# Hyena filters made in the modulation's stage and kept in DRAM until the convolutions

## The reference

```python
def hyena_kernel_fft(L, fw1, fb1, freq, fw2, fb2, fw3):
    hdn = jnp.sin(freq * (feats @ fw1 + fb1))
    hdn = jnp.sin(freq * (hdn @ fw2 + fb2))
    h = (hdn @ fw3).reshape(L, HY_ORDER, 2, HY_W)
    h = h * jnp.exp(-t[:, :, None, None] * jnp.abs(deltas))
    k = jnp.concatenate([h[:, :, 0], zeros, h[:0:-1, :, 1]], axis=0)
    k = k / (jnp.sum(jnp.abs(k), axis=0, keepdims=True) + EPS)
    return jnp.fft.rfft(k, axis=0)

def token_mixer(h, ...):
    u = centred_dwconv(h @ w_in[:, :HY_PROJ], ...); v, *gates = jnp.split(u, 3, axis=-1)
    kf = hyena_kernel_fft(L, ...)
    z = v
    for o, gate in enumerate(gates):
        z = gate * (fft_conv(z, kf[:, o]) + z * hy_bias[o])
    ...

mod = jax.nn.silu(c) @ w_ada + b_ada        # six parts of 2048; also for c_ctx
hc = rmsnorm(h_ctx, norm1_w) * (1.0 + csc1) + csh1
hl = rmsnorm(x, norm1_w) * (1.0 + sc1) + sh1
```

## Time and profile before

| | us |
|---|---|
| median of 3 runs | 4280.64 |
| lowest, highest | 4276.46, 4289.01 |
| the profiled execution | 4285.37 |
| its span, first to last instruction | 4283.6 |
| PE busy | 3877.2 (91%) |
| VectorE busy | 2815.2 (66%) |
| ScalarE busy | 2064.3 (48%) |
| GpSimd busy | 203.6 (5%) |

### The profile page before, as it was taken

The page is one execution under the profiler, slowest core; times in us unless marked ns, Lnnn a source line. Parts: engine busy times, 40 slices in busy tenths (PEclk is TensorE's granted clock), DMA queues, the critical chain, the costliest instruction groups (busy, mean ns, idle before and its releaser), DMA issues. The chain is left out here.

```text
span 4283.6 us, 66352 instructions
## 1 busy us (share of the span) xinstructions
PE 3877.2 (91%) x22156; PEld 3171.7 (74%) x22156; DVE 2815.2 (66%) x5280; ACT 2064.3 (48%) x3828; POOL 203.6 (5%) x242
## 2 busy tenths in 40 slices
PE   6699968778999999887699998998799999999998
PEld 0467744567888888774588877877688888888887
DVE  0553435777888667679686557687966666666667
ACT  0442330235666555455455434444955555555554
POOL 3011100000000000103100000000000000000000
PEclk9899979988999999998899999999999999999999
DMA  9686720034766666441255535555066665666665
GB/s 340 230 302 248 264 92 0 1 106 152 214 214 211 190 188 189 153 150 60 99 177 185 180 110 167 168 184 184 5 200 205 203 203 186 188 189 187 190 189 159
DMA packets 199380, 735.10 MB, mean 172 GB/s; under 512 B 22903, under 2 KB 22936, under 8 KB 197400
## 3 DMA queue, kind: packets, MB, share of 16 engines
q1 hardware_dynamic: 173992, 639.97, 47.6%
q0 software_dynamic: 25200, 92.64, 5.9%
HBM read 715.74 MB, written 16.78 MB: 171 GB/s over the span
## 5 line engine op out<-in xcount | busy, mean ns | idle before, releaser
L207 DVE TENSOR_TENSOR weights_lo<-ring,weights_hi 128x512 fp32r<-128x512 f32 x2240 | 1528.0, 695 | 978.1 <-ACT weights_hi L200 962.5
L200 ACT ACTIVATE weights_hi<-ring 128x512 fp32r<-128x512 f32 x2240 | 1396.4, 630 | 1373.9 <-PE ps L846 1308.4
L846 PE MATMUL ps<-expert_parts,weights_hi 128*128 128x512 f32 x4224 | 1466.9, 395 | 34.3 <-DVE weights_lo L207 26.8
L846 PE MATMUL ps<-expert_parts,weights_lo 128*128 128x256 f32 x4224 | 1142.6, 281 | 0.0
L846 PEld LDWEIGHTS ps<-expert_parts,weights_hi 128*128 128x128 f32 x4224 | 780.7, 189 | 205.2 <-issue 36.4
L846 PEld LDWEIGHTS ps<-expert_parts,weights_lo 128*128 128x128 f32 x4224 | 797.7, 189 | 20.4
L846 PE MATMUL ps<-mlp_parts,weights_hi 128*128 128x512 f32 x1024 | 354.0, 394 | 16.7 <-PEq L604 15.8
L846 PE MATMUL ps<-hidden,weights_hi 128*128 128x512 f32 x1024 | 351.5, 392 | 0.6 <-DVE weights_lo L207 0.6
L846 PE MATMUL ps<-mlp_parts,weights_lo 128*128 128x256 f32 x1024 | 277.4, 281 | 0.0
L846 PE MATMUL ps<-h_parts,weights_hi 128*128 128x512 f32 x704 | 266.1, 406 | 11.8 <-DVE weights_lo L207 11.8
L846 PE MATMUL ps<-hidden,weights_lo 128*128 128x256 f32 x1024 | 276.3, 280 | 0.0
(11 more groups left out here) (460 smaller groups left out, 4972.7 us busy)
## 6 DMA issues: line engine op xcount, KB each, us to landing
ring<-in_w_mlp SPq DMA_DIRECT2D x256, 512.0 KB, 3.7
ring<-in_w_u SPq DMA_DIRECT2D x256, 512.0 KB, 4.1
ring<-in_w_v_tab SPq DMA_DIRECT2D x256, 512.0 KB, 3.7
ada_ring<-in_w_ada POOLq DMA_DIRECT2D x124, 512.0 KB, 6.5
ring<-in_w_mix SPq DMA_DIRECT2D x88, 512.0 KB, 5.6
ada_ring<-in_w_ada SPq DMA_DIRECT2D x68, 512.0 KB, 5.2
ring<-in_w_out SPq DMA_DIRECT2D x64, 512.0 KB, 3.7
ring<-in_w_in SPq DMA_DIRECT2D x48, 512.0 KB, 4.0
```

What stands on the lines that cost most here:

```text
L200: act.activation(core.hi[:, g % SLOTS], core.ring[:, slot, at:at + QUARTER], ACT.Copy).then_inc(core.rounded, 1)
L207: dve.tensor_tensor(core.lo[:, g % SLOTS], core.ring[:, slot, at:at + QUARTER], core.hi[:, g % SLOTS].bitcast(F32), ALU.subtract).then_inc ...
L846: mm = pe.matmul(out, part[:, g % SLOTS, k, :], moving, start=at == 0 and part is core.hi, stop=last and part is core.hi)
```

## The change

The filters move from their own stage, between `dt_stage` and the convolutions, into `start_stage`, and are kept in a DRAM tensor until the convolutions.

- `FilterWork` holds the filter's work. Its loads (feats, w1, w2, w3 of both orders, window, dft) are issued on GpSimd's queue ahead of the other five. PE's part is a generator of 30 pieces: two for the network, then per order two of taps (four matmuls each, into PSUM banks 0 to 3, the second waiting until VectorE has windowed the first), two sums of magnitudes (banks 7 and 0) and ten spectra (banks 1 to 3 in turn). `first_steps` says after which of the 32 steps of the modulation each piece runs. VectorE's part is as before. ScalarE does sines, magnitudes and the copies of the modulation, and issues five stores of 512 KB per order (`spill`) to `filters_saved`, those of order 0 behind the copy of part 0, those of order 1 behind the copy of part 1.
- The buffers lie in space that later stages use: two tiles of 8192 columns, and parts of `u`, `xbc`, `xbc_ctx` and `zg`. ctx now lies in `u`, and the squares' scratch has a tile of its own. ScalarE waits at the stage's end for the stores of order 0 and, before its first work of the projections (`first_scalar`), for those of order 1.
- The block that loaded dft and inverse and `filter_stage` are gone; so is ScalarE's copy of one plane (L1097). In `dt_stage` SyncE issues two transfers of 1 MB from `filters_saved` into the modulation's ring (`early`). In the first `hyena_stage` it issues dft, two planes of 512 KB, inverse, and six planes of order 1 (`rest`). PE waits for dft ahead of its spectra and for inverse ahead of its way back, VectorE for the order's filters ahead of its products.

```diff
 class ModulationBeside(Beside):
+    def first_scalar(self, act):
+        self.filt.wait_spilled(act, 1)
...
-def start_stage(core, mod, ctx_tile, const_loads, scratch, squares):
+def start_stage(core, mod, ctx_tile, const_loads, scratch, squares, filt):
+    first_steps = (2, 5, 8, 9, 11, 12, 13, 13, 14, 15, 15, 16, 17, 17, 18, 19, 20, 21, 23, 24, 25, 25, 26, 27, 27, 28, 29, 29, 30, 31)
+    due = lambda n: sum(at <= n for at in first_steps)
...
-            for part in range(2):
-                mod.copy(act, part)
+            filt.sines(act)
+            filt.sizes(act, 0)
+            mod.copy(act, 0)
+            filt.spill(act, 0)
+            filt.sizes(act, 1)
+            mod.copy(act, 1)
+            filt.spill(act, 1)
+            filt.wait_spilled(act, 0)
         def _(pool):
+            filt.load(pool)
...
+            dve.wait_ge(loaded, 16)
+            filt.vector(dve)
             for part in range(2):
                 mod.finish(dve, part, 1)
...
         def _(pe):
+            pieces = filt.tensor(pe)
+            def after_step(n):
+                for _ in range(due(n) - due(n - 1)):
+                    next(pieces)
             for k in range(KD):
                 mod.multiply(pe, 0, k)
+                after_step(k)
             pe.wait_ge(tables, 16 * (3 + len(const_loads)))
             for k in range(4):
                 mod.multiply(pe, 1, k)
+                after_step(KD + k)
             mod.turn(pe, 0)
             for k in range(4, KD):
                 mod.multiply(pe, 1, k)
+                after_step(KD + k)
+            for _ in pieces:
+                pass
             mod.turn(pe, 1)
...
+class FiltersBack:
+    def early(self, sp):
+        back = self.filters_back[0]
+        sp.dma_start(self.ring[:, 0:2], self.saved[0, :, 0:2]).then_inc(back, 16)
+        sp.dma_start(self.ring[:, 2:4], self.saved[0, :, 3:5]).then_inc(back, 16)
+    def rest(self, sp):
+        dram = self.core.dram
+        sp.dma_start(self.dft[:], dram["dft"]).then_inc(self.dft_back, 16)
+        for n, plane in ((0, 2), (1, 1)):
+            sp.dma_start(self.pairs[0][KN0][:, n], self.saved[0, :, plane]).then_inc(self.filters_back[0], 16)
+        sp.dma_start(self.inverse[:], dram["inverse"]).then_inc(self.inverse_back, 16)
+        for first, n, plane in ((KA0, 0, 0), (KA0, 1, 1), (KN0, 0, 2), (KN0, 1, 1), (KB0, 0, 3), (KB0, 1, 4)):
+            sp.dma_start(self.pairs[1][first][:, n], self.saved[1, :, plane]).then_inc(self.filters_back[1], 16)
...
+    def tensor(self, pe):
...
+        for o in range(2):
+            if o:
+                pe.wait_ge(s["stored"], 2 * self.KINDS)
+            for t in range(TT):
+                if t:
+                    pe.wait_ge(s["windowed"], TT * o + t)
+                for a in range(2):
+                    for c in range(2):
+                        mm = pe.matmul(ps[:, 2 * a + c, :], space.hdn[:, t * P:(t + 1) * P],
+                                       space.w3[o][:, a, c * BANK:(c + 1) * BANK], start=True, stop=True)
+                mm.then_inc(s["taps"], 1)
+                yield
+            pe.wait_ge(s["tapped"], o + 1)
+            for c, bank in enumerate((7, 0)):
+                pe.wait_ge(s["abs"], 2 * o + c + 1)
+                for j in range(4):
+                    mm = pe.matmul(ps[:, bank, :], core.ones[:], space.tmp[:, j, :], start=j == 0, stop=j == 3)
+                mm.then_inc(s["abs_sum"], 1)
+                yield
...
+                for c in range(2):
+                    m = 2 * n + c
+                    if m >= 3:
+                        pe.wait_ge(s["stored"], 2 * self.KINDS * o + m - 2)
...
+                    mm.then_inc(s["spectrum"], 1)
+                    yield
+    def spill(self, act, o):
+        for n, plane in enumerate(self.space.planes[o]):
+            act.wait_ge(self.done["stored"], 2 * self.KINDS * o + 2 * n + 2)
+            act.dma_start(self.saved[o, :, n], plane).then_inc(self.spilled[o], 16)
...
 def hyena_stage
...
                 pe.wait_ge(s["token"], after["token"] + 4)
+                pe.wait_ge(back.dft_back, 16)
...
+                pe.wait_ge(back.inverse_back, 16)
...
+            @block.sync
+            def _(sp):
+                if o == 0:
+                    back.rest(sp)
...
+                dve.wait_ge(back.filters_back[o], back.landings[o])
```

More of the change, by code:

```diff
@@ L920, in dt_stage @@
         with nc.Block() as block:
+            @block.sync
+            def _(sp):
+                back.early(sp)
             @block.tensor
@@ new lines, with __init__ @@
+class FilterSpace:
+    def __init__(self, first, second, u, xbc, zg, xbc_ctx):
+        planes = lambda t: t.rearrange("p n t -> p (n t)")
+        self.taps = first[:, 0:4 * HY].rearrange("p (t a c) -> p t a c", t=TT, a=2)
+        self.tmp = first[:, 4 * HY:6 * HY].rearrange("p (j c) -> p j c", j=4)
+        self.norm = first[:, 6 * HY:7 * HY]
+        self.w1, self.w2 = first[0:33, 7 * HY:7 * HY + 64], first[0:64, 7 * HY + 64:7 * HY + 128]
+        self.hdn = first[0:64, 7 * HY + 128:7 * HY + 128 + T]
+        self.window = second[:, 0:TT * HY].rearrange("p (t c) -> p t c", t=TT)
+        self.dft = second[:, 2 * HY:2 * HY + TT * 6 * P].rearrange("p (t n m) -> p t n m", t=TT, n=6)
+        split = lambda t: t[0:64].rearrange("p (a c) -> p a c", a=2)
+        ctx_planes = planes(xbc_ctx)
+        self.w3 = split(second[:, 4 * HY:6 * HY]), split(ctx_planes[:, 0:2 * HY])
+        pair = lambda t: planes(t).rearrange("p (t c) -> p t c", t=TT)
+        self.even = pair(u[:, 16:24, :]), pair(zg)
+        self.planes = ([second[:, 6 * HY:7 * HY], second[:, 7 * HY:8 * HY], planes(xbc[:, 2:6, :]),
+                        self.even[0][:, 0], self.even[0][:, 1]],
+                       [ctx_planes[:, n * HY:(n + 1) * HY] for n in range(3)] + [self.even[1][:, 0], self.even[1][:, 1]])
@@ new lines, with __init__, make_room @@
+class FiltersBack:
+    def __init__(self, core, saved, ring):
+        self.core, self.saved, self.ring = core, saved, ring
+        self.dft_back, self.inverse_back = core.sem("dft_loaded"), core.sem("inverse_loaded")
+        self.filters_back = [core.sem(f"filters_back{o}") for o in range(2)]
+    def make_room(self, sb):
+        self.dft, self.inverse = sb("dft", [P, TT, 6, P]), sb("inverse", [P, 4, T])
+        last, later = sb("filters_last", [P, 2, HY]), sb("filters_later", [P, 6, HY])
+        self.pairs = ({KA0: self.ring[:, 0:2], KB0: self.ring[:, 2:4], KN0: last[:]},
+                      {n: later[:, n:n + 2] for n in (KA0, KN0, KB0)})
+        self.landings = 64, 96
+    def early(self, sp):
[10 more added lines that the diff above has]
+            sp.dma_start(self.pairs[1][first][:, n], self.saved[1, :, plane]).then_inc(self.filters_back[1], 16)
@@ L1139, in hyena_stage @@
-def hyena_stage(core, o, u, dft, inverse, filters):
+                        ins = dve.tensor_tensor(h[:, t, a, at], ps[:, 2 * a + c, :], space.window[:, t, at], ALU.mult)
+                ins.then_inc(s["windowed"], 1)
+            dve.wait_ge(s["windowed"], TT * (o + 1))
+            dve.memset(h[0:1, 0, 1, :], 0.0).then_inc(s["tapped"], 1)
+            dve.wait_ge(s["tapped"], o + 1)
+            dve.tensor_tensor(even, h[:, :, 0, :], h[:, :, 1, :], ALU.add).then_inc(s["even_odd"], 1)
+            dve.wait_ge(s["abs"], 2 * o + 2)
@@ new lines, in vector @@
+            dve.tensor_tensor(h[:, :, 1, :], h[:, :, 0, :], h[:, :, 1, :], ALU.subtract).then_inc(s["even_odd"], 1)
+            for c, bank in enumerate((7, 0)):
+                at = slice(c * BANK, (c + 1) * BANK)
+                dve.wait_ge(s["abs_sum"], 2 * o + c + 1)
+                step(dve.tensor_scalar(norm[:, at], ps[:, bank, :], EPS, None, ALU.add))
+                step(dve.reciprocal(norm[:, at], norm[:, at]))
+            for n, plane in enumerate(space.planes[o]):
+                for c in range(2):
+                    m = 2 * n + c
+                    at = slice(c * BANK, (c + 1) * BANK)
+                    dve.wait_ge(s["spectrum"], 2 * self.KINDS * o + m + 1)
+                    dve.tensor_tensor(plane[:, at], ps[:, 1 + m % 3, :], norm[:, at], ALU.mult).then_inc(s["stored"], 1)
@@ L1142, in hyena_stage @@
+def hyena_stage(core, o, u, back):
     nc, ps = core.nc, core.ps
@@ L1546, in first_block @@
+                back = FiltersBack(core, filters_saved, mod.ring)
+                dt_stage(core, wdt, h_parts, ctx_parts, ssd, xbc, xbc_ctx, back)
+            with ExitStack() as hyena:
+                back.make_room(lambda name, shape: hyena.enter_context(nc.sbuf_tensor(name, shape, F32)))
+                for o in range(2):
+                    hyena_stage(core, o, u, back)
         h = sb("h_mixed", [P, KD, T])
```

236 lines of the change are left out of this document (96 added, 140 removed).

## The result

The kernel after takes 4229.8 us (median of four runs, 4223.0 to 4232.9), where the kernel before took 4282.0 (median of four, 4276.5 to 4289.0): ratio 0.9874, 95% interval 0.9861 to 0.9887. The predicted 4201 is 29 us too low, and the time lies 8 us above the upper end of the range. For the profiled execution the forecast was 4205, and it took 4229.7: some 24.5 us of the miss stand there. The rest is mostly that the profiled execution before was 4.7 us above its median, while the one after lies on its median.

The account below looks back on a forecast made before the run. It took the first stage as paced by transfers with PE, VectorE and ScalarE idle, and the filter stage as a chain with idle queues. -114.8 + 34.7 = -80.1 us from 4280.6 gave 4200.5, stated as 4201, range 4180 to 4222.

Parts of the forecast that it names:

- Removed side: Between dt stage and convolution: the filter stage and its loads go, 116.8 us less 2 us for the clock, 114.8 us saved.
- the 2 us for the clock: At the first convolution's spectra: loss taken for a cold PE, between nothing and 14 us.
- The way back: Filters returning from DRAM for the convolutions: cost zero, hidden behind spectra; at most 5 us if uncovered.
- By bytes: First stage: new loads add 8.1 us to every later block and the spill of order 0 adds 7.8, together 15.9 us.
- PE paces from step 9 on: First stage: 100.0 us of PE work and waits after step 8, not the queue, make the stage 34.7 us longer.
- the 0.85 named as a sign: First stage, 45 to 150 us: DMA share would fall from 0.94 to about 0.85.
- all at the high clock: First stage, PE's sum: taps 14.2 us, spectra 35.0 and sums of magnitudes 14.2, priced at the high clock.
- a bound for cold spectra: Convolution's spectra: from the first taps run's 14.02 us, all 32 records at half speed would lose at most 14 us.
- The rival of the low clock: First stage: clock falls in six waits (10 us), spill meets ring (4), stage +49, convolution 3 more; 4218 us, chance 0.14.
- 20 us of slack for the transfers: First stage from step 9 on: transfers need 71.7 plus 7.8 us, less than PE's 100, leaving 20 us of slack.
- VectorE and ScalarE cost nothing otherwise: First stage: filter work on these two engines adds nothing beyond the summed waits and tail, as both stood idle.
- the forecast's own range: Whole kernel: stage longer by 27 to 43 us, time 4192 to 4210 us, chance 0.6.

## Why the prediction was wrong where it was

- **Removed side: right in its mechanism, and close by luck.** 114.8 forecast, 115.0 measured. From the dt stage to the first spectrum 116.6 us went, where 116.8 were forecast. The transposes took 3.58 us and the spectra lost nothing, as in the second convolution, so the 2 us for the clock were not needed. In their place the unchanged work elsewhere took 1.6 us longer. That this rest agrees to 0.2 us is chance, since it moved by 15 us between kernels that do the same in it. The Trainium skill, TensorE: Matmul & The Clock Gate, Part 4, has it that transposes don't bring the high clock. This trace disagrees a second time: right behind the transposes the 32 records took 13.97 us.
- **The way back: right.** Nothing waited for the planes.
- **By bytes: 3.3 us too little.** Step 8 ended at 55.5, forecast 52.1. The forecast priced the new bytes at the 370 GB/s of the first 21 us; up to the end of step 8 the transfers moved 336 GB/s, where they had moved 347 before. Other kernels with the same loads had this end at 53.0 to 55.3.
- **PE paces from step 9 on: right.** The DMA share of 45 to 150 us was 0.63, below the 0.85 named as a sign, since the stage took longer. PE's waits for ada_ring, 97.4 us in the earlier trace rows, are now

```profile
PEld ps L377 <- DMA ada_ring<-in_w_ada: 46.5, 22, 6.0
```

  and 42.6 of these 46.5 us stand before the first taps.

- **The step that failed: "all at the high clock".** The sum had 14.2 us for the taps, 14.2 for the magnitudes and 1.0 for each step. Measured were 24.2, 19.0 and, for five steps behind slow taps, 9.0 in place of 5.0: 18 us more, because the clock fell in the pauses and the taps' 64 rows kept it low. Half of this stood in the earlier trace rows and was used for another purpose: the first run of taps, 14.02 us, served as a bound for cold spectra and not as a price for taps behind a wait. Nothing in those rows says that the rows of the operands matter; but two durations for one instruction, 14.02 and 7.10, called for both prices in the sum. The magnitudes were priced by the taps' fast run, though the trace of before has them, and slow. The first order's:

```profile
635.59 6.33 PE L1070 MATMUL ps<-filt_tmp,ones 128*128 128x512 f32 x8 [8.18 <-ACT filt_tmp L1094]
643.92 5.40 PE L1070 MATMUL ps<-filt_tmp,ones 128*128 128x512 f32 x8 [2.00 <-ACT filt_tmp L1094]
```

  The four sums of before took 23.8 us together, where the forecast had 14.2.
- **The rival of the low clock: right mechanism, term too small.** It had six waits at 1.7 us, 10 in all, plus 4 for the stores, and 49 for the stage. Measured: 18 for the clock, 3 for the stores, 59 in all. It let each wait cost a bit of one piece; with 64 rows a piece mostly runs at half speed to its end and hands the low clock to the steps behind it.
- **Stores beside the ring: cost 3 us** where PE's sum had nothing, trusting to 20 us of slack for the transfers. The slack is one of the whole stage; where the stores stood, the DMA engines had none (1.01 busy), and the weight loads waited 0.7 to 0.9 us for second blocks. The rows had no store beside loads.
- **VectorE beside GpSimd: not in the sum.** "VectorE and ScalarE cost nothing otherwise, since both stood idle there" overlooked that GpSimd's sums of squares run at the time of the sine. It cost 1.2 us of wait, and the pause from which the clock fell: in the run with GpSimd late the first taps took 3.70.
- **The range** let only one of these go wrong at a time. A slip besides: the forecast's own range, stage +43 us, gives 4209 and not 4210.

## What to carry to other kernels

When matmuls are moved, price each group at both clocks and ask what stands ahead of it in its new place: here the second price was in the trace already, as two durations for one instruction. Short operands (here 64 rows) are worth padding to 128 where PE paces and pauses stand ahead of them. Zeros on 64 partitions brought the end of the stage forward by 9.0 us alone, 8.3 with the filler, 5.2 with the earlier schedule and 2.3 with GpSimd late. A wait that can't be moved can be filled with matmuls whose result nobody reads: eight records per order gave 5.3 us. An engine that "stood idle" is free only if its neighbour on the same memory ports is idle too: look at GpSimd's lines of the same time. Slack in transfers is that of the stretch and not of the stage.

## What was not expected of the hardware

- Eight records of the same length behind the same pause of 1.6 to 1.7 us: 3.70 us in twelve of twelve cases with 128 rows; with 64 rows 4.57 to 7.18 in seven of eight, and 3.70 in one. Sixteen behind a stretch of little work: 8.85 and 14.02 (granted clock 0.83 and 0.50). 64-row records do run at the high clock when busy PE and no pause stand ahead of them (3.70 at 120.75). Why the rows count is not shown.
- Small VectorE instructions of 0.29 to 0.42 us lasted as long as the GpSimd instruction beside them, up to 4.55 us, while VectorE's windowing, which reads PSUM, took 2.48 us for four beside GpSimd's sums (at 63.98) as without. It goes both ways: where a vector instruction with two inputs of 128x2048 met them, GpSimd's three sums took 12.1 us in place of 8.3.
- Steps of PE beside stores of 512 KB took 1.9 to 2.1 us instead of 1.06 at a granted clock of 1.00. The matmul records show no wait for DMA within a step; the weight loads do, 0.7 to 0.9 us ahead of each second block.
